# Gate and up of a second layer as seven block products instead of eight, with block sums on GpSimd

## What is computed

```python
x = x + gt2 * swiglu(modulate(rms_norm(x, norm2_g[l]), sh2, sc2), w_ffn_gate[l], w_ffn_up[l], w_ffn_down[l])
```

## Time and profile before

| | |
|---|---|
| median of 3 runs | 2487.55 us (2486.88 to 2488.23) |
| the profiled execution: its own time | 2488.97 us |
| its span, first to last instruction | 2487.1 us |
| mean granted TensorE clock | 0.989 |
| busy: PE, DVE, ACT, POOL | 2392.8, 1561.1, 1123.4, 159.6 us |
| attention's output ends, hidden units begin | about 1624.6 us |
| second layer's feed-forward ends | about 2002 us |

### The profile page before, as it was taken

One profiled execution on the slowest core, in us unless ns is written; L12 is line 12 of the kernel. 1 busy time (PEld: TensorE's weight loads), 2 busy tenths in 40 slices (PEclk: granted clock), 3 DMA queues, 4 the chain that ended last, 5 costly groups with the idle time before them and its releaser, 6 DMA issues.

```text
span 2487.1 us, 34523 instructions
## 1 busy us (share of the span) xinstructions
PE 2392.8 (96%) x13215; PEld 2038.5 (82%) x13215; DVE 1561.1 (63%) x2454; ACT 1123.4 (45%) x1776; POOL 159.6 (6%) x283
## 2 busy tenths in 40 slices
PE   7999999999999999999999999999999999998898
PEld 3888877788888888888778877799998977777677
DVE  5776777788666554454686777644443566377763
ACT  5647777723321121122647775332222355566541
POOL 0200000110000000000100001000000010011010
PEclk9999999999999999999999999999999999999999
DMA  7411111363333333322221113423232333421253
GB/s 280 154 65 46 51 39 45 121 234 122 145 135 122 131 121 136 119 77 85 94 85 52 52 52 113 149 87 100 86 100 86 103 115 134 159 79 61 83 196 110
DMA packets 67961, 268.88 MB, mean 108 GB/s; under 512 B 8432, under 2 KB 8496, under 8 KB 66528
## 3 DMA queue, kind: packets, MB, share of 16 engines
q1 hardware_dynamic: 42336, 162.94, 19.0%
q0 software_dynamic: 25472, 103.82, 11.9%
HBM read 238.42 MB, written 27.26 MB: 107 GB/s over the span
## 4 chain that ended last, share of the span: by engine, by line
PE 79%; DVE 9%; ACT 6%; issue 4%; DMA 2%; POOL 0%; SPq 0%; ACTq 0%; DVEq 0%
PE ps L189 22%; PE ps L191 22%; PE ps L190 22%; DVE w_lo L185 1%; PE ps L1201 1%; PE ps L1202 1%; PE ps L1203 1%; PE ps L1135 1%; DMA w_raw<-in_stream 1%; PE ps L1142 1%; DMA ada_raw<-in_ada 1%; DVE inv L1362 1%; PE ps L1184 1%; ACT w_hi L178 1%; PE ps L2063 1%
## 5 line engine op out<-in xcount | busy, mean ns | idle before, releaser
L189 PE MATMUL ps<-h_hi,w_hi 128*128 128x512 f32 (+2 forms) x2680 | 916.3, 342 | 16.7 <-DVE h_lo L1501 6.4
L191 PE MATMUL ps<-h_hi,w_lo 128*128 128x512 f32 (+2 forms) x2680 | 905.9, 338 | 0.0
L190 PE MATMUL ps<-h_lo,w_hi 128*128 128x512 f32 (+2 forms) x2680 | 905.5, 338 | 0.0
L189 PEld LDWEIGHTS ps<-h_hi,w_hi 128*128 128x128 f32 x2680 | 507.6, 189 | 81.3 <-issue 17.3
L191 PEld LDWEIGHTS ps<-h_hi,w_lo 128*128 128x128 f32 x2680 | 508.5, 190 | 57.3
L190 PEld LDWEIGHTS ps<-h_lo,w_hi 128*128 128x128 f32 x2680 | 507.8, 189 | 56.3 <-issue 2.4
L185 DVE TENSOR_TENSOR w_lo<-w_raw,w_hi 128x1024 fp32r<-128x1024 f32 x288 | 351.9, 1222 | 171.4 <-ACT w_hi L178 171.1
L178 ACT ACTIVATE w_hi<-w_raw 128x1024 fp32r<-128x1024 f32 x288 | 302.8, 1052 | 302.8 <-PE ps L191 284.3
L189 PE MATMUL ps<-q_hi,w_hi 128*128 128x512 f32 x720 | 255.9, 355 | 1.4 <-DVE q_lo L1522 1.4
L191 PE MATMUL ps<-q_hi,w_lo 128*128 128x512 f32 x720 | 256.4, 356 | 0.0
L190 PE MATMUL ps<-q_lo,w_hi 128*128 128x512 f32 x720 | 256.2, 356 | 0.0
(11 more groups left out here) (359 smaller groups left out, 3062.4 us busy)
## 6 DMA issues: line engine op xcount, KB each, us to landing
w_raw<-in_stream SPq DMA_DIRECT2D x288, 512.0 KB, 3.5
wt<-in_ada_t POOLq DMA_DIRECT2D x72, 512.0 KB, 3.8
ada_raw<-in_ada SPq DMA_DIRECT2D x4, 2048.0 KB, 18.0
x_keep<-x POOLq DMA_DIRECT2D x8, 768.0 KB, 7.0
gates<-th_g POOLq DMA_DIRECT2D x16, 384.0 KB, 2.6
x<-x_keep POOLq DMA_DIRECT2D x2, 3072.0 KB, 13.0
gates<-sg POOLq DMA_DIRECT2D x24, 256.0 KB, 2.3
wt_q<-in_ada_t POOLq DMA_DIRECT2D x8, 512.0 KB, 3.8
```

The costliest lines, as they stand in the source:

```text
L189: nc.tensor.matmul(out_ap, lh, rh, start=start, stop=False)
L190: nc.tensor.matmul(out_ap, lh, rl, start=False, stop=False)
L191: return nc.tensor.matmul(out_ap, ll, rh, start=False, stop=stop)
```

## The change

For the second layer alone, `hidden_halved` takes the place of `hidden_late`. The pair's 256 rows (gate, up) and its 1024 inputs are halved, and so are the tokens: A = (a11 a12; a21 a22), B = (b11 b12; b21 b22). Seven products of 4 chunks x 3 matmuls, with 258 or 256 columns, replace eight: a11 b11, a12 b21, s2 t2, s1 t1, s3 t3, s4 b22, a22 t4, where s and t are sums of blocks: s1 = a21 + a22, s2 = s1 - a11, s3 = a11 - a21, s4 = a12 - s2, and likewise for t.

- POOL makes the four sums of weight halves of each pair from the raw units (`half_sums`), and in the attention's output units four sums of token blocks per two chunks (`sums`). It also multiplies both results with the root row (`root`), which DVE did.
- ACT and DVE split seven halves of 512 per pair in place of two units of 1024 (`half_hi`, `half_lo`), four halves ahead, in six half slots.
- The evictions recombine: ACT copies the first product (`s1`), DVE has four additions that read PSUM (after products 3, 5, 6, 7), ACT adds the up bias (`up_bias`).
- In the attention's output units (now in the order 0, 4, 1, 5, ...) each two chunks of `x` are scaled to `hs`, then seven blocks of 256 tokens are split to high and low in place of one chunk's `h_hi` and `h_lo`; the last six blocks come after the last unit.
- SP loads into four buffers in place of two in this stretch.

The diff, cut to its core:

```diff
--- before.py
+++ after.py
...
+HALVES = ("a11", "a12", "s2", "s1", "s3", "s4", "a22")
...
+def ticks(units):
+    return units + 5 * sum(u < units for u in SEVEN)
...
+        def half_source(u, k):
+            name, n = HALVES[k], SEVEN[u] * P
+            if name[0] == "s":
+                return w_sum[:, int(name[1]) - 1, 0:n]
+            at = n * (int(name[2]) - 1)
+            return raw_home(u + int(name[1]) - 1)[:, at:at + n]
+        def half_hi(act, u, k):
+            name = HALVES[k]
+            if name[0] == "s":
+                act.wait_ge(sums_ready.sem, sums_ready.base + 4 * PAIR_NUMBER[u] + int(name[1]))
+            else:
+                raw_here(act, u + int(name[1]) - 1)
+            act.wait_ge(unit_done, 1 + WEIGHT_FREED[u, k])
+            nc.scalar.activation(half_of(w_hi, u, k), half_source(u, k), ACT.Copy).then_inc(hi_ready, 1)
+        def half_lo(dve, u, k):
+            dve.wait_ge(hi_ready, ticks(u) + k + 1)
+            nc.vector.tensor_tensor(half_of(w_lo, u, k), half_source(u, k), half_of(w_hi, u, k).bitcast(F32),
+                                    ALU.subtract).then_inc(lo_ready, 1)
+        def half_sums(pool, u):
+            n, was = SEVEN[u] * P, PAIR_NUMBER[u]
+            g, up_ = raw_home(u), raw_home(u + 1)
+            s = [w_sum[:, i, 0:n] for i in range(4)]
+            raw_here(pool, u)
+            raw_here(pool, u + 1)
+            for i, (a, b, op) in enumerate([(up_[:, 0:n], up_[:, n:2 * n], ALU.add), (s[0], g[:, 0:n], ALU.subtract),
+                                            (g[:, 0:n], up_[:, 0:n], ALU.subtract), (g[:, n:2 * n], s[1], ALU.subtract)]):
+                if was:
+                    before = [v for v in SEVEN if PAIR_NUMBER[v] == was - 1][0]
+                    pool.wait_ge(lo_ready, ticks(before) + HALVES.index(f"s{i + 1}") + 1)
+                if i in (1, 3):
+                    pool.wait_ge(sums_ready.sem, sums_ready.base + 4 * was + i)
+                nc.gpsimd.tensor_tensor(s[i], a, b, op).then_inc(sums_ready.sem, 1)
...
+            if u - u % 2 in SEVEN:
+                for k in (0, 1) if u % 2 == 0 else (2, 3):
+                    half_hi(act, u - u % 2, k)
+                return
...
+        class Halved(Late):
...
+            steps = ("b11", "b21", "t2", "t1", "t3", "b22", "t4")
...
+            def sums(self, pool, u):
+                def of(i):
+                    (a1, b1), (a2, b2) = ((self.hs[i % 2][:, g, 0:256], self.hs[i % 2][:, g, 256:512]) for g in range(2))
+                    t = [self.t_sum[:, i % 2, k, :] for k in range(4)]
...
+                    nc.gpsimd.tensor_tensor(t[0], b1, a1, ALU.subtract).then_inc(self.full.sem, 1)
...
+                    nc.gpsimd.tensor_tensor(t[1], b2, t[0], ALU.subtract).then_inc(self.full.sem, 1)
+                    nc.gpsimd.tensor_tensor(t[2], b2, b1, ALU.subtract).then_inc(self.full.sem, 1)
...
+                    nc.gpsimd.tensor_tensor(t[3], a2, t[1], ALU.subtract).then_inc(self.full.sem, 1)
+                of(0)
+                of(1)
+                half_sums(pool, u)
+                of(2)
+                of(3)
...
+        def hidden_halved(nf, late, before, opening):
+            nonlocal u0
+            base = u0
...
+            P1, P4, P3 = ps[:, 1, 0:258], ps[:, 4, 0:258], ps[:, 6, 0:256]
+            P2, P6 = ps[:, 2, 0:258], ps[:, 3, 0:258]
+            P5, P7 = ps[:, 7, 0:256], ps[:, 7, 256:512]
+            home = (P1, P2, P6, P5, P7, P3, P4)
+            su = lambda p: cu[:, p % 2, 0:2, 0:256]
+            ff = lambda p: cu[:, p % 2, 3:5, 0:256]
+            halves = lambda row: row.rearrange("p (g n) -> p g n", g=2)
...
+            def pe(e):
+                def product(p, k, chunks=range(4)):
+                    u = unit(p)
+                    high_, low_, n = late.blocks[Halved.steps[k]]
+                    wh, wl = half_of(w_hi, u, k), half_of(w_lo, u, k)
+                    if chunks[0] == 0:
+                        e.wait_ge(lo_ready, ticks(u) + k + 1)
...
+                    for c in chunks:
+                        if opening and p == 0:
+                            e.wait_ge(late.low.sem, late.low.base + 2 + 7 * c + k + 1)
+                        w = slice(c * P, c * P + P)
+                        mm = three(home[k], wh[:, w], wl[:, w], high_[:, c, 0:n], low_[:, c, 0:n], c == 0, c == 3)
+                    if chunks[-1] == 3:
+                        mm.then_inc(unit_done, 1)
+                for p in range(nf):
+                    if opening and p == 0:
+                        for k in range(3):
+                            product(p, k, range(3))
+                        for k in range(3):
+                            product(p, k, range(3, 4))
+                        late.statistic(e)
+                        product(p, 3)
+                        product(p, 4)
+                        late.spread(e)
...
+                    for k in range(7):
+                        product(p, k)
+            def act(e):
+                def up_bias(p):
+                    e.wait_ge(read.sem, read.base + 4 * p + 4)
+                    nc.scalar.activation(cu[:, p % 2, 3, 256:257], P4[:, 256:257], ACT.Identity,
+                                         bias=cu[:, p % 2, 2, 256:257]).then_inc(biased.sem, 1)
+                def silu(p):
+                    e.wait_ge(times_root.sem, times_root.base + 2 * p + 1)
+                    nc.scalar.activation(su(p), su(p), ACT.Silu, bias=cu[:, p % 2, 0, 256:257]).then_inc(silud.sem, 1)
+                def split(p):
+                    e.wait_ge(gated.sem, gated.base + p + 1)
+                    nc.scalar.activation(halves(q_hi[:, p, 0:SEQ]), ff(p), ACT.Copy).then_inc(high.sem, 1)
...
+                for b in range(N):
+                    p, k = b // 7, b % 7
+                    if p and k == 0:
+                        up_bias(p - 1)
+                    if b + 4 < N:
+                        half_hi(e, unit((b + 4) // 7), (b + 4) % 7)
+                    elif b == N - 3:
+                        split_hi(e, unit(nf))
+                    elif b == N - 1:
+                        split_hi(e, unit(nf) + 1)
+                    if k == 0:
+                        done(e, p, 0)
+                        if p:
+                            e.wait_ge(read.sem, read.base + 4 * (p - 1) + 1)
+                        nc.scalar.activation(s1[:, :], P1, ACT.Copy).then_inc(copied.sem, 1)
...
+                    if p and k == 1:
+                        silu(p - 1)
+                    if p and k == 3:
+                        split(p - 1)
+                up_bias(nf - 1)
+                silu(nf - 1)
+                split(nf - 1)
+            def dve(e):
+                def evict(p, k):
+                    j = p % 2
+                    u2 = cu[:, j, 2, 0:256].unsqueeze(1).to_broadcast([P, 2, 256])
+                    if k == 2:
+                        done(e, p, 2)
+                        e.wait_ge(copied.sem, copied.base + p + 1)
+                        nc.vector.tensor_tensor(cu[:, j, 0:3:2, :], ps[:, 2:4, 0:258], s1[:, :].unsqueeze(1).to_broadcast([P, 2, 258]),
+                                                ALU.add).then_inc(read.sem, 1)
+                    if k == 4:
+                        done(e, p, 4)
+                        e.wait_ge(read.sem, read.base + 4 * p + 1)
+                        nc.vector.tensor_tensor(u43[:, :, :], halves(ps[:, 7, :]), u2, ALU.add).then_inc(read.sem, 1)
+                    if k == 5:
+                        done(e, p, 5)
+                        e.wait_ge(read.sem, read.base + 4 * p + 2)
+                        nc.vector.tensor_tensor(cu[:, j, 1:5:3, 0:256], ps[:, 6:8, 0:256], u43[:, :, :], ALU.add).then_inc(read.sem, 1)
+                    if k == 6:
+                        done(e, p, 6)
+                        nc.vector.tensor_tensor(cu[:, j, 3, 0:256], P4[:, 0:256], u43[:, 1, :], ALU.add).then_inc(read.sem, 1)
+                def gate(p):
+                    e.wait_ge(silud.sem, silud.base + p + 1)
+                    e.wait_ge(times_root.sem, times_root.base + 2 * p + 2)
+                    e.wait_ge(biased.sem, biased.base + p + 1)
+                    nc.vector.scalar_tensor_tensor(ff(p), ff(p), cu[:, p % 2, 3, 256:257], su(p), ALU.add, ALU.mult).then_inc(gated.sem, 1)
+                def split(p):
+                    e.wait_ge(high.sem, high.base + p + 1)
+                    nc.vector.tensor_tensor(halves(q_lo[:, p, 0:SEQ]), ff(p), halves(q_hi[:, p, 0:SEQ]).bitcast(F32),
+                                            ALU.subtract).then_inc(low.sem, 1)
+                for b in range(N):
+                    p, k = b // 7, b % 7
+                    if b + 4 < N:
+                        half_lo(e, unit((b + 4) // 7), (b + 4) % 7)
+                    elif b == N - 3:
+                        split_lo(e, unit(nf))
+                    elif b == N - 1:
+                        split_lo(e, unit(nf) + 1)
...
+                    evict(p, k)
```

(28 more changed lines are left out.)

326 lines of the change are left out of this document (268 added, 58 removed).

## The result

The changed kernel takes 2520.61 us (median of 4 runs, 2514.58 to 2526.24); the kernel before took 2487.89 us beside it. The ratio is **1.013, 95% interval 1.0103 to 1.0158**: slower by 1.3%. The median is 10.6 us above the forecast of 2510 and inside the forecast's own range for case A (2500 to 2533). The profiled execution took 2517.59 us; its span is 28.6 us longer than the span before, while the medians differ by 32.7 us.

The account below looks back on a forecast made before the run. The prediction took PE's work to bound the second layer's hidden units. Its terms, -31.5 + 56.5 - 12 + 6 + 3 = +22.0 on the profiled 2488.97, gave 2511.0, with the runs' median 1.4 lower: 2510 us, range 2458 to 2540.

Parts of the forecast that it names:

- case A: Steady pairs: DVE with two SBUF inputs and POOL exclude each other; pair 12.6 us, kernel 2500 to 2533; chance 0.60.
- PE, -31.5: Hidden-unit pairs: 84 matmuls in place of 96, 10.03 us a pair in place of 11.46; -31.5 us over 22 pairs.
- DVE and ACT fit alone: Steady pairs: DVE's work of 7.7 us and ACT's of 5.4 us each fit into PE's 10.03 us.
- Exclusion, pair 12.6, +56.5: Steady pairs: DVE and POOL block each other over SBUF reads; pair 12.6 us against 10.03, +56.5 us (bounds 0 and +98).
- with half of the cover lost, pair 13.5: Steady pairs: if half of the evictions' overlap with POOL is lost, a pair takes 13.5 us and the kernel 2530.
- Lead -12: Start of each of three parts: four halves split ahead delay PE's waiting; 4 us per part, -12 us (bounds -17 and 0).
- ends of parts +6: End of each part: DVE's last work, 5.2 us, outlasts the first down unit's cover; +6 us (2 to 10).
- Opening +3 (0 to 6): Attention's output units: subtractions covered, but last sums and splits precede the root, 5.4 us against PE's 4.3; +3 us.
- That PE's clock falls in the new gaps is no case of its own: PE's new gaps: no separate clock loss, since a pair at 12.6 us keeps PE at 80%, in gaps of about a us.
- B: Steady pairs: DVE's second SBUF read and POOL don't meet, so the kernel gets faster, 2460 us; chance 0.24.
- C: Steady pairs: only POOL is held, DVE never; POOL needs 9.2 us, under 10.03; kernel 2462 to 2478; chance 0.10.
- D: Steady pairs: no exclusion, but ACT and DVE wait on each other without overlap, 11.4 us; kernel 2487, no change; chance 0.06.

Follow-up runs that it names:

- The kernel with the bias later: Against the changed kernel, ACT's copy of the up bias moved from ahead of a weight split to behind it; 2521.04 us, ratio 1.0134.
- the same edit of order: ACT's up-bias copy put behind a weight split: 2521.04 us on the changed kernel, 2502.73 with root products on DVE, 2494.18 with weight sums there too.

## Why the prediction was right, and where it was off

- **PE, -31.5:** right. 264 matmuls fewer, and without holds a pair takes 9.98 us (forecast 10.03).
- **DVE and ACT fit alone:** right (POOL's work taken away: 9.98 us, `w_lo` 689 ns, gate 745).
- **Exclusion, pair 12.6, +56.5:** the mechanism is shown by five kernels: without reads on POOL no cost (two of them); all its work gone from the steady pairs and DVE's own grown, `w_lo` still at 686 and 684 ns (two); a sum laid beside instructions that read PSUM, one hold gone. The size was low: 13.17 us, 22 x (13.17 - 10.03) = +69. The step that failed is "if the only cover are the four evictions": I let all 2.2 us of evictions lie under POOL's six instructions. In the timeline after two of the four do (1673.16 and 1679.31, 1.1 us together); the others come while POOL is idle. The prediction had this case too, "with half of the cover lost, pair 13.5", and the measured pair lies nearer to it than to 12.6. Counted on DVE, the lengthening of 4.6 us is near the forecast's 12.6 - 7.7 = 4.9; what the forecast had at nothing is the idle 0.85 us beside it. The kernel with the bias later shows that the two trade: there the idle time goes and the lengthening is 5.4.
- The forecast leaned on a rule of the Trainium skill (SBUF — State Buffer, section Who interferes with whom), that VectorE with two SBUF inputs contends with a GpSimd instruction that reads SBUF. The runs agree for sums and products (`w_lo` 1.10 to 1.26 us beside them in the mean, evictions from PSUM 0.68), for copies (`w_lo` held to 1.05 us), and for memsets, which don't read (0.69 us). The other half, that one SBUF input doesn't contend, agrees for instructions with a second input in PSUM (0.68 us beside POOL). The page states it outside VectorE's two-port modes only, which the prediction left out; `pr` in rows 6, with one SBUF input and none in PSUM, did meet POOL, and POOL waited.
- **Lead -12 and ends of parts +6:** together -6. What is left for them is 28.6 - 1.2 + 5.2 + 31.5 - 69.1 - 8.9 = -13.9; it is a remainder and not a measurement. The ends alone, in PE's waits, are 8.0 for `q_lo` and 2.5 for `w_lo` of 1024, just over the forecast's upper bound of 10, so the lead must be larger than forecast. A part of it is known: each part's last pair took 11.03 us in place of 13.17, as POOL has no next pair to sum for, 3 x 2.14 = 6.4 us.
- **Opening +3 (0 to 6):** measured 8.9, outside the bounds. The working behind it, 5.4 less PE's 4.3, gives 1.1; for the rest of the +3 no reason was given. Two steps failed. The first is "that is covered", of the out units' subtractions. Timeline of DVE there, after:

```profile
1614.80 1.52 DVE L674 TENSOR_TENSOR t_lo<-t_sum,t_hi 128x256 fp32r<-128x256 f32 x1
1616.24 1.22 DVE L512 TENSOR_TENSOR acc<-acc,sq 128x512 f32<-128x512 f32 x1
1617.39 0.74 DVE L1888 SCALAR_TENSOR_TENSOR x<-ps,vec,x 128x512 f32<-128x512 f32 x1
```

  This subtraction of 256 and the one before it take 1.52 us each where 0.41 is usual, the running sum 1.22 where it takes 0.68 one unit later, and the `x` add comes 2.6 us late; the stage lost 2.2 us. DVE's own work was covered; POOL's sums beside it were not counted as holds there, though the same rule was applied to the pairs. It is the first pair's four weight sums, placed in this stage, that cost: the three kernels in which these are memsets or copies keep the token sums and take 39.20 us for the stage, as before, and all others 41.34 to 41.37. The second step is the chained sums between the last unit and the root: with POOL's work taken away the first pair's last eviction comes 1639.68 - 1625.63 = 14.05 us after the last add, with it 18.59, before 13.3. Corrected by the 1.43 of the missing product that is +2.2 and +6.7: the +3 was about right for a kernel without the weight sums' holds.
- **"That PE's clock falls in the new gaps is no case of its own":** right for the pairs (1.00 in the pair shown above), wrong for the opening. Length, busy us of PE, PEld, DVE, ACT, POOL, clock, DMA, after:

```profile
1630.00:1633.00 3.00, 1.48 (x6) 1.27 (x6) 2.45 (x3) 2.83 (x8) 3.00 (x4) 0.77 0.00 0
1633.00:1636.00 3.00, 0.40 (x2) 0.10 (x1) 3.00 (x5) 2.74 (x5) 1.76 (x2) 0.50 0.00 0
1636.00:1639.00 3.00, 2.49 (x11) 2.49 (x12) 3.00 (x4) 0.55 (x3) 1.72 (x2) 0.50 0.00 0
1639.00:1642.00 3.00, 3.00 (x17) 3.00 (x16) 2.76 (x8) 0.95 (x2) 1.51 (x1) 0.53 0.54 132
```

  The granted clock falls while PE has 1.9 of 6 us of work, and is then at 0.50 to 0.53, the lower level of 1.2 GHz, over 9 us. With POOL's work taken away PE has a gap too, of 1.3 us, but the clock stays:

```profile
1630.00:1633.00 3.00, 1.68 (x13) 1.47 (x14) 2.70 (x7) 2.99 (x5) 0.10 (x1) 1.00 0.00 0
1633.00:1636.00 3.00, 3.00 (x28) 3.00 (x28) 2.90 (x9) 1.64 (x5) 0.10 (x1) 1.00 0.29 68
```

  By PE's 5.9 busy us from 1633 to 1642 the low clock costs some 3 of the 8.9 us; that is an estimate from the rows, no run separates it.
- **Not forecast:** -5.2 us behind the feed-forward. At the last norm PE's clock was at 0.63, 0.50 and 0.73 in three stretches of 3 us from 2008 before; after, in four from 2035.8, it was at 1.00, 0.90, 0.53 and 1.00. As the other kernels with the seven products don't show the 5.2 us, it looks like a trait of this one execution and not an effect of the change; no run was made for it.
- **Rivals.** B and C fell by the trace (`w_lo` isn't at 0.69; both engines are held, not POOL alone). D as put (full durations in the ring, 11.4 us) is contradicted by the kernel without POOL's work, 9.98. But a ring with idle time behind ACT is real as soon as the holds go: 0.53 us a pair with four sums on POOL, 0.83 (12.57 - 11.74) with none.

The terms as measured: -31.5 + 69.1 + 8.9 - 13.9 + 1.2 - 5.2 = +28.6. The forecast's total was nearer than its terms, which was in part luck: 12.6 too little for the pairs and 5.9 for the opening stand against -7.9 of lead and ends and -4.0 of two terms that the change doesn't explain.

What stays open: the same GpSimd load beside the kernel before, where DVE has slack, was not tried; nor was a version without the gate's last hold.

## What to carry to other kernels

Work that is moved to an idle engine is not free: compare the durations of the neighbours, by form, before and after. In these runs a GpSimd instruction that reads SBUF and a VectorE instruction with two SBUF inputs take turns, so the price is set by what stands beside what: a few sums on GpSimd, laid beside VectorE's reads of PSUM, are worth it, a train of six is not. Take holds away before tuning an order; the same edit of order was worth 0 us under the train of six, 9.5 with four sums and 17.6 with none. A mean over a group can hide a hold: the copies looked harmless by their mean, and single `w_lo` beside them were 0.4 us too long.

## What was not expected of the hardware

- A GpSimd memset of 512 columns (0.53 us) holds nothing on VectorE. A copy (0.83 to 0.88 us) holds a `w_lo` to 1.1 us at most and cost the pair 0.06 us; a sum or product of two inputs (1.4 to 1.7 us beside VectorE, 1.30 where it meets instructions that read PSUM) holds it to 1.8 us at most, and six of them cost the pair 0.53 us each.
- A held VectorE instruction ends 0.54 to 0.56 us after the GpSimd one, however long it was held, `w_lo` and gate alike, beside sums and copies alike: this is so in each of nearly 400 held instructions in seven traces. It looks as if its data passed only when the other is through; the traces show the time alone.
- The times of one kernel spread more than four runs show: the kernel before spread over 2.7 us beside the changed one, and over 11.7 and 14.0 us in the two comparisons with 19 and 12 runs of it.
